# Eight merge-gate tiles in pieces inside the attention's units

## The reference

```python
out = lax.map(block_fn, (jnp.arange(nq), q_blocks))          # sparse attention, softmax per branch
y_nsa = nsa_attention(q, kc, vc, ks, vs, kw, vw, gates)
g = jax.nn.sigmoid(mgate).reshape(B, T, N_BRANCH, D_MODEL)   # mgate = h @ w_in[..., 3072 columns]
m = (g[:, :, 0] * (y_hg @ w_br_hg) + g[:, :, 1] * (y_gla @ w_br_gla)
     + g[:, :, 2] * (y_nsa @ w_br_nsa))
return m @ w_out
```

## Time and profile before

| | us |
|---|---|
| timed runs (3), median | 3135.19 |
| lowest and highest | 3129.74, 3136.34 |
| the profiled execution, its own time | 3131.34 |
| its span, first to last instruction | 3129.3 |
| PE busy | 3070.3 |
| DVE busy | 1500.4 |
| ACT busy | 724.5 |
| POOL busy | 1901.0 |

### The profile page before, as it was taken

One profiled execution on the slowest core, in us unless ns is written; L12 is line 12 of the kernel. 1 busy time (PEld: TensorE's weight loads), 2 busy tenths in 40 slices (PEclk: granted clock), 3 DMA queues, 4 the chain that ended last, 5 costly groups with the idle time before them and its releaser, 6 DMA issues.

```text
span 3129.3 us, 41325 instructions
## 1 busy us (share of the span) xinstructions
PE 3070.3 (98%) x15116; PEld 2462.6 (79%) x15116; DVE 1500.4 (48%) x2613; ACT 724.5 (23%) x1461; POOL 1901.0 (61%) x885
## 2 busy tenths in 40 slices
PE   8999999999999999999999999999999999999998
PEld 6678888868888888876688888888787668888887
DVE  4564430465552143886645454114388664544411
ACT  4420100441100123435501110022343550111000
POOL 4277777537777876001288777787600128877776
PEclk9899999999999999999999999999999999999999
DMA  3133222213322322112032322322211202233222
GB/s 124 48 107 96 94 100 94 75 41 108 101 94 96 100 87 88 48 35 82 21 100 96 101 94 97 98 96 93 82 48 37 79 28 95 95 101 100 95 95 86
DMA packets 71713, 262.29 MB, mean 84 GB/s; under 512 B 8208, under 2 KB 8208, under 8 KB 71440
## 3 DMA queue, kind: packets, MB, share of 16 engines
q1 hardware_dynamic: 71280, 258.34, 25.4%
q10 hardware_dynamic: 288, 1.98, 0.2%
HBM read 258.20 MB, written 2.10 MB: 83 GB/s over the span
## 4 chain that ended last, share of the span: by engine, by line
PE 85%; DVE 6%; issue 4%; POOL 3%; ACT 2%; DMA 0%; SPq 0%; DVEq 0%; POOLq 0%; ACTq 0%
PE bank L650 83%; POOL w_hi L1417 1%; POOL w_lo L1425 1%; PE bank L1281 1%; DVE arena L1995 1%; DVE bank L1995 1%; DVE rope L1995 1%; PE bank L665 0%; DVE arena L2366 0%; DVE rope L1992 0%; ACT act_hi L1572 0%; ACT arena L1917 0%; DVE w_lo L2392 0%; DVE x L1995 0%; DVE arena L1992 0%
## 5 line engine op out<-in xcount | busy, mean ns | idle before, releaser
L1417 POOL TENSOR_TENSOR w_hi<-ring,one 128x1024 fp32r<-128x1024 f32 x430 | 817.0, 1900 | 1156.5 <-PE bank L650 573.1
L1425 POOL TENSOR_TENSOR w_lo<-ring,w_hi 128x1024 fp32r<-128x1024 f32 x422 | 1039.3, 2463 | 40.4 <-DVE h_lo L2019 7.6
L650 PE MATMUL bank<-h_hi,w_hi 128*128 128x512 f32 x2256 | 895.5, 397 | 3.4 <-POOL w_lo L1425 3.4
L650 PE MATMUL bank<-h_hi,w_lo 128*128 128x512 f32 x2256 | 880.9, 390 | 0.0
L650 PE MATMUL bank<-h_lo,w_hi 128*128 128x512 f32 x2256 | 880.5, 390 | 0.0
L650 PE MATMUL bank<-act_hi,w_hi 128*128 128x512 f32 (+1 forms) x1376 | 506.1, 394 | 5.1 <-POOL w_lo L1425 2.7
L650 PEld LDWEIGHTS bank<-h_hi,w_hi 128*128 128x128 f32 x2256 | 424.2, 188 | 97.7 <-issue 5.1
L650 PEld LDWEIGHTS bank<-h_hi,w_lo 128*128 128x128 f32 x2256 | 424.0, 188 | 91.1
L650 PEld LDWEIGHTS bank<-h_lo,w_hi 128*128 128x128 f32 x2256 | 424.3, 188 | 85.3 <-issue 1.0
L650 PE MATMUL bank<-act_hi,w_lo 128*128 (+1 forms) x1120 | 437.5, 391 | 0.0
L650 PE MATMUL bank<-act_lo,w_hi 128*128 (+1 forms) x1120 | 421.0, 390 | 1.4 <-DVE act_lo L2598 1.4
(11 more groups left out here) (249 smaller groups left out, 2850.5 us busy)
## 6 DMA issues: line engine op xcount, KB each, us to landing
ring<-wstream SPq DMA_DIRECT2D x480, 512.0 KB, 3.5
par<-params SPq DMA_DIRECT2D x4, 529.5 KB, 4.5
x<-xT SPq DMA_DIRECT2D x4, 512.0 KB, 7.5
outT<-h SPq DMA_DIRECT2D x4, 512.0 KB, 2.7
cst<-const ACTq DMA_DIRECT2D x1, 1412.0 KB, 8.7
par<-params ACTq DMA_DIRECT2D x1, 525.5 KB, 5.1
arena<-pos SPq DMA_DIRECT2D x1, 256.0 KB, 2.6
cst<-const SPq DMA_DIRECT2D x1, 24.5 KB, 2.4
```

The costliest lines, as they stand in the source:

```text
L650: return pe.matmul(out, lhsT, rhs, start=start, stop=stop)
L1417: return po.tensor_tensor(out, a, one.broadcast_to([P, n]), ALU.mult)
L1425: po.tensor_tensor(pair_[1], raw, pair_[0].bitcast(F32), ALU.subtract).then_inc(done.sem, 1)
```

## The change

`HELD` = 14: gate tiles 6 to 13 are multiplied inside the attention's units, each in pieces of blocks, all in bank 1; ACT copies each out raw, and takes the sigmoids later. Gate 14 stands in two parts of four blocks between the last transposes. `MERGE` becomes gates 6 to 17, branches 0 to 8, gates 18 to 23, branches 9 to 11, and the stream's tiles are reordered to match. So between the attention and the first branch product three gate tiles (15, 16, 17) are left where there were four (8 to 11). All value products use bank 0, so that `pair_pv` waits for the copy of the pair before. Waits and buffers follow: the held gates lie in `sig0`, `rope1`, `rope2`, `rstd` and two places of the arena, the merging products use two other places, POOL's wait for the second unit's scaling goes, and ACT makes six high parts of the merged sum after gate 17 in place of four and, after gate 20, two. The core of the diff:

```diff
+        HELD = 14
-        MERGE = [("gate", n) for n in range(EARLY, 12)] + [("branch", n) for n in range(6)] + \
-                [("gate", n) for n in range(12, 18)] + [("branch", n) for n in range(6, 9)] + \
+        MERGE = [("gate", n) for n in range(EARLY, 18)] + [("branch", n) for n in range(9)] + \
                 [("gate", n) for n in range(18, 24)] + [("branch", n) for n in range(9, 12)]
...
-        mg_c = later(mx_sd, EARLY + 1)
+        mg_c = later(mx_sd, HELD)
...
         def gate_bank(n):
-            return bank[1] if n == EARLY else bank[(0, 6, 7)[(n - EARLY - 1) % 3]]
+            return bank[1] if n < HELD else bank[(1, 6, 7, 0)[(n - HELD) % 4]]
+        def held_gate(n):
+            if n < EARLY:
+                return m2["sig0"][:, n, :]
+            return (gate_raw, rstd[:, 0, :], rstd[:, 1, :], rope1[:, 0, :], rope1[:, 1, :], ropec, ropes,
+                    view(25248, T))[n - EARLY]
+        def sigmoid_gate(n):
+            if n < HELD:
+                return m2["sig"][:, 0, :] if n == EARLY else held_gate(n)
+            return m2["sig"][:, n % 6, :]
...
-                    if win == 0 and 0 in blocks:
-                        if j == 1:
-                            pe.wait_ge(*mg_c(l, EARLY + 1))
-                        elif j >= 2:
-                            pe.wait_ge(*no_y(l, j - 1))
+                    if win == 0 and 0 in blocks and j > 0:
+                        pe.wait_ge(*no_y(l, j))
...
-                        if n == EARLY + 1:
-                            pe.wait_ge(*no_y(l, 3))
-                        elif EARLY + 1 < n < EARLY + 4:
+                        if EARLY < n <= HELD:
+                            pe.wait_ge(*mg_c(l, n))
+                        elif HELD < n < HELD + 3:
                             pe.wait_ge(*ns_od(l, 16))
-                        elif n >= EARLY + 4:
-                            pe.wait_ge(*mg_s(l, n - 2))
+                        elif n == HELD + 3:
+                            pe.wait_ge(*no_y(l, 4))
+                        elif n > HELD + 3:
+                            pe.wait_ge(*mg_s(l, n - 3))
...
+                def held_part(w, blocks):
+                    if 1 <= w <= HELD - EARLY:
+                        merge_gate(w - 1, EARLY + w - 1, blocks)
                 pair_scores(steps_of(0))
-                merge_gate(0, EARLY, range(4))
+                held_part(1, range(3))
                 for w in range(1, 9):
                     steps = steps_of(w)
                     pair_scores(steps[0:1])
+                    held_part(w - 1, (6, 7))
                     pair_turn(w - 2, 1)
                     pair_scores(steps[1:2])
                     pair_turn(w - 2, 2)
-                    if w == 1:
-                        merge_gate(0, EARLY, range(4, ND))
+                    if w > 1:
+                        held_part(w, (0, 1))
...
                     pair_pv(w - 2, (0, 1))
                     pair_scores(steps[2:3])
+                    held_part(w, (2, 3) if w > 1 else (3,))
                     pair_pv(w - 2, (3,))
                     pair_scores(steps[3:4])
                     pair_pv(w - 2, (2,))
+                    held_part(w, (4, 5))
                     pair_turn(w - 1, 0)
-                for g, part in enumerate(((0, 1, 2), (3, 4, 5), (6, 7))):
-                    if g > 0:
-                        pair_turn(7, g)
-                    merge_gate(1, EARLY + 1, part)
+                held_part(8, (6, 7))
+                for g, part in ((1, (0, 1, 2, 3)), (2, (4, 5, 6, 7))):
+                    pair_turn(7, g)
+                    merge_gate(HELD - EARLY, HELD, part)
...
-                    elif i == 2:
-                        po.wait_ge(*ns_c(l, 2))
...
-                    if w == 1:
-                        sc.wait_ge(*mg_mm(l, EARLY + 1))
-                        sc.activation(gate_raw, gate_bank(EARLY)[:, :], ACT.Copy).then_inc(mg_c.sem, 1)
...
+                            if g == 0 and w <= HELD - EARLY:
+                                k = EARLY + w - 1
+                                sc.wait_ge(*mg_mm(l, k + 1))
+                                sc.activation(held_gate(k), gate_bank(k)[:, :], ACT.Copy).then_inc(mg_c.sem, 1)
...
                 for n in range(EARLY + 1):
+                    held_sigmoid(n)
                 sc.wait_ge(*mg_s(l, EARLY + 1))
                 for c in range(12):
                     sc.wait_ge(*(lo_n(l, c + 1) if c < 8 else no_y(l, c - 7)))
                     sc.activation(branch_hi[c], branch_raw[c], ACT.Copy).then_inc(yb_h.sem, 1)
+                for n in range(EARLY + 1, HELD):
+                    held_sigmoid(n)
...
-    out += [gates[1], prods[0], prods[1], gates[2], prods[2], gates[3], prods[3]]
+    out += [gates[1], gates[2], prods[0], prods[1], prods[2], gates[3], prods[3]]
```

More of the change, by code:

```diff
@@ L1298, in pair_pv @@
                         for e in range(2):
-                            last = product(bank[j % 2][64 * e:64 * e + 64, st * P:T], m2["nv"][:, st, at:at + 64],
+                            last = product(bank[0][64 * e:64 * e + 64, st * P:T], m2["nv"][:, st, at:at + 64],
                                            nprobT[e][:, PT0[st]:PT0[st] + (NT - st) * P], win == 0 and st == 0, False)
@@ L1304, in pair_pv @@
                             rows = slice(32 * (hd % 4), 32 * (hd % 4) + NCMP)
-                            last = product(bank[j % 2][64 * e:64 * e + 64, :],
+                            last = product(bank[0][64 * e:64 * e + 64, :],
                                            m2["vc"][rows, (j // 2) * 64:(j // 2) * 64 + 64],
@@ L1376, in mixer2 @@
                         merge_branches(i, n)
-                    elif i > 1:
+                    elif n > HELD:
                         merge_gate(i, n)
@@ L1907, in pair_out @@
                     sc.wait_ge(*ns_v(l, 2 * j + 2))
-                    sc.activation(m2["nq"][:, j, :], bank[j % 2][:, :], ACT.Copy).then_inc(no_y.sem, 1)
+                    sc.activation(m2["nq"][:, j, :], bank[0][:, :], ACT.Copy).then_inc(no_y.sem, 1)
                 for w in range(10):
@@ L1933, in mixer2, with held_sigmoid @@
                                     .then_inc(ns_o.sem, 1)
+                            if g == 0 and w <= HELD - EARLY:
+                                k = EARLY + w - 1
+                                sc.wait_ge(*mg_mm(l, k + 1))
+                                sc.activation(held_gate(k), gate_bank(k)[:, :], ACT.Copy).then_inc(mg_c.sem, 1)
                 pair_out(3)
+                def held_sigmoid(n):
+                    sc.wait_ge(*mg_c(l, n + 1))
+                    sc.activation(sigmoid_gate(n), held_gate(n), ACT.Sigmoid).then_inc(mg_s.sem, 1)
                 for n in range(EARLY + 1):
-                    sc.wait_ge(*mg_c(l, n + 1))
-                    raw, out = (m2["sig0"][:, n, :],) * 2 if n < EARLY else (gate_raw, m2["sig"][:, 0, :])
-                    sc.activation(out, raw, ACT.Sigmoid).then_inc(mg_s.sem, 1)
+                    held_sigmoid(n)
                 sc.wait_ge(*mg_s(l, EARLY + 1))
@@ L1942, in mixer2 @@
                     sc.activation(branch_hi[c], branch_raw[c], ACT.Copy).then_inc(yb_h.sem, 1)
+                for n in range(EARLY + 1, HELD):
+                    held_sigmoid(n)
                 def gate_out(n):
                     sc.wait_ge(*mg_mm(l, n + 1))
-                    if n >= 2 * EARLY:
+                    if n >= 18:
                         sc.wait_ge(*br_m(l, n - 5))
-                    sc.activation(m2["sig"][:, n % 6, :], gate_bank(n)[:, :], ACT.Sigmoid).then_inc(mg_s.sem, 1)
+                    sc.activation(sigmoid_gate(n), gate_bank(n)[:, :], ACT.Sigmoid).then_inc(mg_s.sem, 1)
                 def merged_high(j):
@@ L1952, in merged_high @@
                     sc.activation(m_hi[j], m2["m"][:, j, :], ACT.Copy).then_inc(wo_h.sem, 1)
-                for n in range(EARLY + 1, 24):
+                for n in range(HELD, 24):
                     gate_out(n)
                     if n == 17:
[L1957 to L1960, removed]
+                        for j in range(6):
                             merged_high(j)
@@ L2602, in mixer2 @@
                     j, b = r // 3, r % 3
-                    sig = m2["sig0" if r < EARLY else "sig"][:, r % 6, :]
+                    sig = sigmoid_gate(r)
                     m = m2["m"][:, j, :]
-                    out = (m, ropec, ropes)[b]
+                    out = (m, view(17408, T), view(17920, T))[b]
                     ve.wait_ge(*mg_s(l, r + 1))
```

## The result

Slower by 0.7%, and by about as much as forecast. The changed kernel took 3154.7 us (median of 6 runs, 3147.58 to 3157.7), the kernel before 3135.11 beside it (6 runs, 3129.74 to 3136.51): ratio 1.0068, interval 1.0054 to 1.0082, that is +21 us (17 to 26). The forecast was 3154, with 23 us added. The profiled execution took 3150.61, its span is 3148.5.

A forecast was written before the change was run, and what follows sets the result against it. PE, busy 98% of the span, was taken to set the time. Per layer 5.4+1.7+3.9+1.1-0.5=11.6 us, 23 for two layers, on the profiled 3131.34 gave 3154; range 3139 to 3162.

The forecast's parts named there:

- The stall, 5.4: Ahead of the third branch product, PE waits for DVE's low parts: 5.4 us lost a layer, bounds 3.5 and 6.
- The clock, 1.7: Behind the idle time at the branches, 3.4 us of PE work at half speed: 1.7 us lost a layer, bounds 0 and 3.4.
- The pieces, net 3.9: In the attention, cutting gate tiles into pieces costs 0.5 us a full unit, net 3.9 a layer, bounds 1.5 and 5.5.
- The first loop's mask, 1.1: In the attention's first loop, score step 8 waits for step 6's mask from DVE: 1.1 us a layer, bounds 0 and 1.5.
- The tail, -0.5: In the attention's last stretch, gate pieces cover PE's waits on ACT's copies: -0.5 us a layer, bounds 0 and -1.5.
- ACT, DVE, POOL and SP, nothing: In the attention's units, added copies, splits and loads on the other engines make nothing late for PE: no cost.
- no stall: Rival: at the branches, DVE's subtractions get past POOL sooner, so 9 us remain: 3140; chance 0.12.
- a clock that stays up: Rival's second half: no slow clock behind the branches' idle time, together with cheaper pieces: 3147; joint chance 0.14.
- Half the pieces' price: Rival's first half: cut gate tiles cost 2 us a layer, with no slow clock: 3147; joint chance 0.14.
- The units' 0.2 are waits: Rival: the 0.2 us at each change of work in the attention's units is waiting that gate pieces fill: 3120; chance 0.06.

The follow-up runs named there:

- Experiments 1 to 3: The first: the kernel before with gate tile 11 moved behind branch tiles 0 and 1; 3146.86 us, ratio 1.0044. Experiment 2 and experiment 3 have their own lines.
- experiment 2: The changed kernel with gate tile 18 ahead of the branch products, so four gate tiles stand there again; 3138.56 us, ratio 1.0023.
- experiment 4: The changed kernel with 22 products that nobody reads put on PE ahead of the third branch product; 3148.44 us, ratio 1.0052.
- experiment 5: The changed kernel with each held gate tile in one piece, between the unit's last transposes and its value products; 3149.65 us, ratio 1.0059.
- experiment 3: The changed kernel with ACT's first five high parts of the branch inputs ahead of its seven sigmoids; 3141.34 us, ratio 1.0023.

## Why the prediction was right

By its own steps, per layer.

- *The stall, 5.4.* 5.43 and 5.45 in the trace of the two layers, on L2593 of before, as named. Experiments 1 to 3 show the reason given: the tile makes it, the fourth tile or earlier low parts undo it. The part of the argument that it rested on, that the low parts hang on the attention's end and not on the gates, came out at 27.69, 27.64 and 27.70 us in before, the changed kernel and experiment 2.
- *The clock, 1.7.* 1.7 and 2.2 (experiment 4). The level and the place were right; the length taken over from the earlier trace rows, 3.4 us, was a little short, since behind the stalls the granted clock stays low for 3.9 and 4.7 us.
- *The pieces, net 3.9.* A full unit was to cost 0.5 and costs 0.43. Over the 1.36 that six products stream, the four pieces of the unit shown cost 0.14, 0.22 less 0.17 at the transposes ahead, 0.25 and 0.14, 0.58 in all where the terms had 0.52. What no term had: eight transposes ahead of scores take 0.96 behind a piece and not 1.02, 0.06 twice; 0.03 lie in scores and value products. Net of the next two terms the attention's 4.0 leaves 4.0-1.03+0.5=3.5, and the second layer's 3.8-1.03+0.8 about 3.5 as well.
- *The first loop's mask, 1.1.* 1.03.
- *The tail, -0.5.* -0.5 and -0.8; the copies of turned probabilities were next, as said, with a wait of 0.49 left.
- *ACT, DVE, POOL and SP, nothing.* In PE's list of waits for the stage, 1440 to 1760 us, no new wait stands beyond those named.

The sum is 11.2 and 11.4 against 11.6. The span grew by 19.2 between the two profiled executions, less than these 22.6, since the changed kernel's reached its first gate tile 4.3 us earlier (1457.97 and 1462.27), in a part of the program that the change leaves alone. The largest difference there is the clock: before had a granted clock of 0.50 from 102 to 115 us, where the other had 1.00, and fell back by 6.4 us over it; smaller differences, most of them the other way, make up the rest. From the gate tile on the span grew by 23.5: 22.6 in the two stages, 1.5 between them, and 0.6 less behind the second.

That the forecast, 3154, meets the measured 3154.7 to a microsecond is partly luck. It starts from one execution at 3131.34, 3.8 below the median of before, and adds 23 where 21 was measured.

Of the rivals, "no stall" and "a clock that stays up" fell by the result itself, with a wait of 5.43 and a granted clock of 0.50 behind it; experiments 2 and 4 show why. "Half the pieces' price" had about 0.25 a unit, where 0.43 was measured. "The units' 0.2 are waits" fell by experiment 5: a whole tile gains nothing, since 13.68 is 8.20, the tile and 0.03.

## What to carry to other kernels

A run of matrix work between two stages is also the time that the other engines have to prepare the next one. Before moving a piece of it, measure from the event that starts the preparation (here the attention's end) to its last instruction, and compare with what PE still has to do: with next to no slack, as here, a tile taken out came back whole as a stall, with the slow clock behind it. And filler put into an engine whose rows name no wait filled nothing here; cut small, it paid at its edges. So put it in whole, where the array's work already changes.

## What the hardware showed beyond that

- The low clock is there when PE starts again; the cost is of the work behind the stall, not of its idle time. 5.4 us idle cost 1.7 and 2.2 more, 0.3 and 0.4 of the stall on top. Twenty-two products that nobody reads were enough to keep it at 1.00.
- The edges of a float32r tile have a price of their own: 0.08 to 0.12 us on the first start and about 0.1 on the last when scores or value products follow, none when transposes follow.
- DVE's subtractions beside POOL's splits: one takes under 0.7 us while POOL is idle (the first five in experiment 3) and up to 2.88 beside a half of a split. Four take 8.53 and 8.58 us beside three halves (the changed kernel and experiment 2) and 10.33 beside four, about one more slow subtraction for a half. No experiment took the splits away from the last four low parts, so what the stall would be without POOL is not shown.
